# RMS norm of x ahead of its transposes: scaling on VectorE and turning by transposes, in place of products with a diagonal matrix

## The reference

```python
def rms_norm(x, g):
    xf = x.astype(jnp.float32)
    y = xf * lax.rsqrt(jnp.mean(xf * xf, axis=-1, keepdims=True) + NORM_EPS)
    return (y * g.astype(jnp.float32)).astype(x.dtype)
...
    x = x + 0.5 * swiglu_ffn(rms_norm(x, ffn1_norm), ffn1_w_gate, ffn1_w_up, ffn1_w_down)
    proj = rms_norm(x, mix_norm) @ w_in
...
    x = x + jnp.concatenate([y_hy, y_mla, y_gla], axis=-1) @ w_out
    x = x + 0.5 * swiglu_ffn(rms_norm(x, ffn2_norm), ffn2_w_gate, ffn2_w_up, ffn2_w_down)
...
    return rms_norm(x, final_norm)
```

## Time and profile before

| | us |
|---|---|
| median of 3 runs | 1053.82 (1053.79 to 1053.95) |
| the profiled execution, device time | 1060.01 |
| its span, first to last instruction | 1058.3 |
| TensorE matmul busy | 1027.3 (97%) |
| VectorE busy | 608.7 (58%) |
| ScalarE busy | 492.5 (47%) |
| GpSimd busy | 105.6 (10%) |
| mean granted TensorE clock | 0.991 |

### The profile page before, as it was taken

How to read it: one execution, slowest core, us unless ns; L and a number is a source line. 1 busy time by engine, 2 the same in 40 slices (tenths; PEclk the granted TensorE clock), 3 DMA queues, 4 the chain that set the end, 5 groups by cost and what they waited for, 6 DMA issues and landing times.

```text
span 1058.3 us, 18037 instructions
## 1 busy us (share of the span) xinstructions
PE 1027.3 (97%) x7060; PEld 931.1 (88%) x7060; DVE 608.7 (58%) x650; ACT 492.5 (47%) x654; POOL 105.6 (10%) x159
## 2 busy tenths in 40 slices
PE   6999999999999999999989999999999999999996
PEld 6999999788678999999989999997886889999995
DVE  4554455577875655455465554547689774554554
ACT  6434434457654534434355344344476554344343
POOL 1000000150522000000010000003325200000000
PEclk9999999999899999999999999999999999999999
DMA  8555555353304545545455455452542235455451
GB/s 313 201 195 197 184 177 194 120 200 120 120 1 160 186 177 193 193 164 198 175 181 182 180 196 187 172 196 80 199 145 95 81 139 215 168 196 188 173 214 40
DMA packets 26117, 177.07 MB, mean 167 GB/s; under 512 B 3120, under 2 KB 3632, under 8 KB 5200
## 3 DMA queue, kind: packets, MB, share of 16 engines
q1 hardware_dynamic: 24912, 174.21, 45.6%
q0 software_dynamic: 720, 1.95, 0.7%
q10 hardware_dynamic: 432, 0.18, 0.1%
HBM read 175.63 MB, written 1.05 MB: 167 GB/s over the span
## 4 chain that ended last, share of the span: by engine, by line
issue 89%; POOL 9%; POOLq 1%; DMA 0%; DVE 0%; ACT 0%; DVEq 0%; SPq 0%
POOL mixer_scratch L319 4%; POOL mixer_scratch L340 1%; POOL mixer_scratch L339 1%; POOL statistics L296 1%; POOL statistics L294 1%; POOL statistics L306 1%; DMA x<-in_x_dram 0%; POOL x_normed L344 0%; POOLq L220 0%; POOL mixer_scratch L341 0%; POOL x_normed L348 0%; POOL statistics L305 0%; POOL statistics L303 0%; DVE x_normed L940 0%; POOL statistics L295 0%
## 5 line engine op out<-in xcount | busy, mean ns | idle before, releaser
L618 DVE TENSOR_TENSOR w_low<-w_raw,w_high 128x2048 fp32r<-128x2048 f32 x163 | 375.1, 2305 | 218.0 <-ACT w_high L378 217.8
L950 PE MATMUL psum<-xT_high,w_high 128*128 128x256 f32 x1536 | 437.0, 285 | 4.7 <-DVE xT_low L623 4.1
L951 PE MATMUL psum<-xT_low,w_high 128*128 128x256 f32 x1536 | 434.6, 283 | 0.0
L952 PE MATMUL psum<-xT_high,w_low 128*128 128x256 f32 x1536 | 434.6, 283 | 0.0
L378 ACT ACTIVATE w_high<-w_raw 128x2048 fp32r<-128x2048 f32 x163 | 311.0, 1914 | 128.4 <-PE psum L952 125.8
L950 PEld LDWEIGHTS psum<-xT_high,w_high 128*128 128x128 f32 x1536 | 294.6, 192 | 8.8 <-DVE xT_low L623 4.9
L951 PEld LDWEIGHTS psum<-xT_low,w_high 128*128 128x128 f32 x1536 | 294.6, 192 | 1.9 <-issue 0.5
L952 PEld LDWEIGHTS psum<-xT_high,w_low 128*128 128x128 f32 x1536 | 294.6, 192 | 0.0
L407 ACT ACTIVATE silu_gate<-psum 128x256 f32<-128x256 f32 x88 | 33.6, 382 | 273.1 <-PE psum L952 273.0
L950 PE MATMUL psum<-w_high,hT_high 128*128 128x512 f32 (+1 forms) x360 | 139.9, 389 | 0.0
L951 PE MATMUL psum<-w_low,hT_high 128*128 128x512 f32 (+1 forms) x360 | 139.7, 388 | 0.0
(11 more groups left out here) (166 smaller groups left out, 768.0 us busy)
## 6 DMA issues: line engine op xcount, KB each, us to landing
w_raw<-in_w_dram SPq DMA_DIRECT2D x163, 1024.0 KB, 4.8
x<-in_x_dram SPq DMA_DIRECT2D x2, 512.0 KB, 4.5
mixer_scratch<-in_fil_dram POOLq DMA_DIRECT2D x2, 512.0 KB, 6.7
out_dram<-x_normed SPq DMA_DIRECT2D x4, 256.0 KB, 2.1
mixer_scratch<-in_fil_dram POOLq DMA_DIRECT2D x2, 352.0 KB, 6.2
mixer_scratch<-in_fin_dram SPq DMA_DIRECT2D x1, 512.0 KB, 5.7
dft<-in_dft_dram SPq DMA_DIRECT2D x1, 256.0 KB, 5.6
inverse_dft<-in_dft_dram SPq DMA_DIRECT2D x1, 256.0 KB, 4.9
```

The source lines that it names most:

```text
L618: e.tensor_tensor(WL[p][:], raw[p][:], WH[p][:].bitcast(F32), ALU.subtract).then_inc(s_lo.sem, 1)
L950: e.matmul(out, ah, bh, start=start, stop=False)
L951: e.matmul(out, ah, bl, start=False, stop=False)
L952: return e.matmul(out, al, bh, start=False, stop=stop)
```

## The change

The diagonal matrix and its buffer go. `scaled` takes the place of `diagonal`, at the same places of DVE's program: it multiplies x itself by the reciprocal norm, two instructions of 128 x 512 for each token tile, into `x_normed`. TensorE's `norm` then turns the blocks of `x_normed` by transposes against the identity, and waits for each quarter of `x_normed` by itself. The semaphore `x_scaled` counts quarters.

```diff
-        diag = sb("diag_rstd", [P, T, P])
...
-            def diagonal(l, j, t):
+            def scaled(l, j, t):
 
                 e.wait_ge(s_rstd.sem, s_rstd.at(l, 2 * j + t + 1))
-                e.tensor_scalar(diag[:, t, :], ident, st[:, T_R + t:T_R + t + 1], float(D) ** 0.5, ALU.mult, ALU.mult).then_inc(s_dg.sem, 1)
+                for n in range(2):
+                    c = slice(n * 512, (n + 1) * 512)
+                    e.tensor_scalar(xn[:, t, c], x[:, t, c], st[:, T_R + t:T_R + t + 1], float(D) ** 0.5, ALU.mult, ALU.mult).then_inc(s_xs.sem, 1)
...
                             if j != 0:
-                                diagonal(l, j + 1, 0)
+                                scaled(l, j + 1, 0)
                             e.wait_ge(s_used.sem, used(l, slot))
...
                 if j != 0:
-                    diagonal(l, j + 1, 1)
+                    scaled(l, j + 1, 1)
...
                 window(0, 0)
-                diagonal(l, 1, 0)
+                scaled(l, 1, 0)
                 window(0, 1)
-                diagonal(l, 1, 1)
+                scaled(l, 1, 1)
...
             def norm(l, j, turn):
                 for t in range(T):
-                    e.wait_ge(s_dg.sem, s_dg.at(l, 2 * j + t + 1))
                     for k in range(KD):
+                        if k % 4 == 0:
+                            e.wait_ge(s_xs.sem, s_xs.at(l, 4 * j + 2 * t + k // 4 + 1))
                         if t == 0 and k == 6:
                             e.wait_ge(s_x.sem, s_x.at(l, 4 * j + 4))
 
-                        r = e.matmul(PS[:, k // 2, (k % 2) * SEQ + t * P:(k % 2) * SEQ + (t + 1) * P], x[:, t, k * P:(k + 1) * P], diag[:, t, :],
-                                     start=True, stop=True)
+                        r = e.transpose(PS[:, k // 2, (k % 2) * SEQ + t * P:(k % 2) * SEQ + (t + 1) * P], xn[:, t, k * P:(k + 1) * P], ident)
                         if t == 1 and k % 2:
                             r.then_inc(s_tr.sem, 1)
```

More of the change, by code:

```diff
@@ L183, in build @@
         s_x = mark("x_updated", 4 * NORMS)
-        s_ss, s_rstd, s_dg = mark("squares_summed", 4 * NORMS), mark("rstd", 2 * NORMS), mark("rstd_diagonal", 2 * NORMS)
+        s_ss, s_rstd, s_xs = mark("squares_summed", 4 * NORMS), mark("rstd", 2 * NORMS), mark("x_scaled", 4 * NORMS)
         s_sum = mark("bank_summed", 3 * NORMS)
@@ L796, in _ @@
             for t in range(T):
-                diagonal(0, 0, t)
+                scaled(0, 0, t)
             lo(0, 0)
```

## The result

| | us |
|---|---|
| before, median of 6 executions | 1053.82 (1053.61 to 1053.95) |
| changed, median of 6 executions | 1065.78 (1061.58 to 1070.2) |
| ratio | 1.0105, 95% interval 1.0079 to 1.0131 |
| the profiled execution of the changed kernel | 1070.12, span 1068.4 |

The kernel became 1.05% slower. The time lies in the forecast's whole range of 1054.6 to 1066.5, 3.5 us above its middle and 0.8 above the range that it gave to four falls alone (1059 to 1065).

What follows compares the result with a forecast made beforehand. TensorE, in flight 97% of the span, was taken as the bound only where it does not wait. From 1053.8 us, +0.95 for VectorE's delays less the n1 gain and +7.6 for four clock falls gave 1062.3, range 1054.6 to 1066.5.

Steps and rivals of the forecast that it cites:

- four falls alone: Clock falls at the first FFN, both n2 and n0 of the second layer: +7.6 us, time 1062.3, chance 0.52.
- Rival (a): The clock stays up at all four places: 1054.8 us, chance 0.19.
- (d): TensorE's saving passes whole at n1 and the clock stays up: 1052.3 us, or 1051.3; chance 0.06.
- (c): The clock falls at only one or two of the four places: 1056.7 to 1058.6 us, chance 0.11.
- Rival (b): Transposes leave TensorE so idle that the clock falls at n1 too, two more falls: 1066.1 us, chance 0.12.
- n2, each: Last quarter's update waits behind the longer scaling, 0.59 us later; shorter transposes return 0.07: +0.5 us each.
- n0 of layer 2: The second scaling starts later and ScalarE starts at 536.02 where it was 535.77: +0.25 us.
- tail: The last update comes 0.59 us later and an unused scaling stands ahead of the output: +1.2 us.
- n1, each: Shorter transposes let TensorE's filter products start 0.75 us earlier; bounds 0 and 2.0; two together -1.5 us.
- The price of a fall: FFN time lost per clock fall at a norm or the start: 1.9 us each, four +7.6, bounds 0 and 9.6.
- The rule of a half: Dense FFN work loses half of its time at the lower clock: 4.8 us there would lose 2.4.
- The fall in the mixer: A chance clock fall in a mixer, 6.08 us in the profile before; left out of the middle, widening the top.

Runs made afterwards that it cites:

- the first three experiments: The changed kernel with fp32 identity products for its transposes (1058.01 us), or with TensorE's waits at norms filled by unused products (1054.92) or unused transposes (1055.00).
- second profiled execution: The changed kernel measured again without any edit, twelve executions for their spread: median 1063.35 us, ratio 1.0062; the profiled one is one of two at 1068.2.

## Why the prediction was right, step by step

**The mechanism** held at all four places it named: the first FFN, n2 twice, n0 of layer 2, each with the clock at 0.50. What shows that the missing activity of TensorE is the cause is the first three experiments: same VectorE work, other work on TensorE, no fall at a norm. Rival (a), no fall, and (d), faster, fell by the result; (c), fewer places, fell since none of the 18 executions of the changed kernel is below 1061.5. Rival (b), falls at n1, fell with the windows at n1: 208 to 212 us above, and 208 to 213 and 730 to 735 us of the changed kernel, all at 1.00. The rule of the Trainium skill that speaks for (b), in "TensorE: Matmul & The Clock Gate", Part 4 (PE-mode transpose), doesn't hold for these fp32 transposes: where transposes alone filled the waits, the kernel took 1055.00, against 1054.92 with products.

**VectorE's terms**, from stretches without a fall:

| term | forecast | measured |
|---|---|---|
| n2, each | +0.5 | +0.51 |
| n0 of layer 2 | +0.25 | +0.35 |
| tail | +1.2 | +1.18 to +1.20 |
| n1, each | -0.75 | -0.87 |
| together | +0.95 | +0.8 |

The sizes came out because the rows before had the same instruction in the same shape, 475 ns, and the changed kernel has it at 475 ns in its smallest case and 479 in the middle one of 28. The chain from there was the old one, moved by the longer stand ahead of the last update. At n1 the forecast gave each quarter 0.7 beside GpSimd. That was right in the sum by luck: three of the four took 0.48 and the last 0.95, the second pair 1.34, and the filter product came 0.73 earlier, as forecast 0.75. The stretch then gained 0.14 more, which I can't place.

**The price of a fall** is the mis-sized term: 1.9 each, +7.6 together. The stretches of the first profiled execution, with VectorE's share taken off, give 2.5 at the start (where other kernels scatter by 0.2), 1.95 and 2.24 at n2 (2.46 and 2.75 less 0.51), 2.6 at n0 (2.93 less 0.35): 9.3. The second profiled execution gives, in the order of time, 2.6, 2.2, 1.3 and 1.2: 7.3. So a price is between 1.2 and 2.6, and the bounds of 0 and 9.6 for four held.

What the forecast had too simple is the length. It took one, 4.8 us, from the start of the kernel before, and half of it as the most that a fall can cost. The traces show how long the FFN ran at the lower level, from its first product to the window in which the clock is back:

| falls | FFN at the lower level | price |
|---|---|---|
| changed, both executions: start, n0 of the first, n2 of layer 2 in the first, n2 of layer 1 in the second | 5.5 to 6.1 | 2.2 to 2.6 |
| n2 of layer 1 in the first; both n2 with n2 alone changed | 4.2 to 4.5 | 1.9 to 1.95 |
| start and n0 with n0 alone changed; n0 and n2 of layer 2 in the second | 3.1 to 3.6 | 1.2 to 1.3 |

The price is 0.37 to 0.45 us for each us of FFN at the lower level, in twelve falls. The rule of a half was a little too high, and the one length of 4.8 lies in the middle of what came.

**The fall in the mixer** I left out of the middle. The first profiled execution has it, 6.07 us, and by their times (1070.2, 1067.78) two more of the first six had one; in the second series two of twelve. So the first median, 1065.78, lies between the executions with it and those without (1061.58, 1063.02, 1063.77). That is most of the 3.5 us between forecast and result. Here luck had a part: three of the six had such a fall, and with a fourth the median would have been above 1066.5, outside the whole range.

**Open:** what sets the length of a fall, whether one comes in a mixer, and why TensorE began n0 of layer 2 late in the kernels with n1 and with n2 changed. No run was made for any of these. The kernel before has 1.00 at that n0, behind a wait of 1.19 us.

## What to carry to other kernels

Before you take work off TensorE near a wait, ask what keeps its clock up there: of the 2.0 us saved at each of six norms 0.9 arrived at two, and the falls that the new idle time brought cost 9.3 us in the first profiled execution and 7.3 in the second. Where TensorE itself is the limit, as at n1, the transpose is a gain; where it waits, fill the wait with work that nobody reads, products or transposes, and put a longer instruction of VectorE behind the update that the next norm's sum waits for. Compare kernels by stretches between equal rows and by all executions: a median of six can differ by 2.4 us from the median of the next twelve.

## What the runs showed that I had not expected

- Fp32 transposes count as activity of TensorE here. At the start of the changed kernel only sixteen of them run before the first weights: the median one takes 421 ns and the shortest 272, and the engine sat idle from 11.3 on. The last two start at 10.95 and 11.06 and take 0.27 us, at the upper level; those that start from 8.2 to 10.5 take 0.42. (The clock column says 1.00 for 10 to 11 all the same: ahead of the first rise it doesn't show the lower level, and only the durations do.) The granted clock fell again in 14 to 15 (0.67), after three idle us. The clock rose on transposes alone, and was lost in the wait.

```profile
L969 PE MATMUL psum<-constants,x_normed x16: 272/421/477, 7.9 to 11.1; 128*128 128x128 f32 x16
...
10.00:11.00 1.00, 1.00 (x7) 1.00 (x6) 0.00 (x0) 0.79 (x1) 1.00 (x2) 1.00 1.08 459
14.00:15.00 1.00, 0.00 (x0) 0.00 (x0) 1.00 (x3) 1.00 (x4) 0.00 (x0) 0.67 1.01 229
```

- The kernel before has not one time but three, near 1053.8, 1058.7 and 1063.6. The profile of before shows one fall in a mixer, at 6.1 us (1060.01); two of the experiments' profiles, with transposes as filling and with the order changed, have one at 4.9 and 4.8, which is the distance between the three times. That none, one and two falls make them is inferred from this size. In the series of 35 executions 24 took under 1055.
- A scaling of 128 x 512 on VectorE takes 475 to 486 ns in 26 of 28 cases, six of them beside GpSimd's additions at n1. The other two take 945 and 950: the last one at each n1, with one of GpSimd's additions of 128 x 256 running beside it and the next behind that. What sets these two apart from the others is open.

```profile
L631 DVE TENSOR_SCALAR x_normed<-x,statistics x28: 475/479/950, 7.4 to 1062.0; 128x512 f32<-128x512 f32 x28
```
